# A streaming encoder step: TensorE's seven rounds of the recurrence as a loop or written out, and the order in which slots of the weight stream are asked for

## The reference

```python
def step(S, inp):
    r_t, d_t, k_t, v_t, kk_t, b_t = inp
    sa = jnp.einsum('bhvk,bhk->bhv', S, kk_t)
    S = S * d_t[:, :, None, :] - sa[..., None] * b_t[:, :, None, :] + v_t[..., None] * k_t[:, :, None, :]
    return S, jnp.einsum('bhvk,bhk->bhv', S, r_t)
```

## Time and profile before

| | us |
|---|---|
| median of 3 runs | 3645.53 |
| lowest, highest | 3642.49, 3646.55 |
| the profiled execution | 3655.61 |
| its span, first to last instruction | 3654.1 |
| TensorE busy in it | 3442.9 |
| VectorE, ScalarE, GpSimd busy | 1739.2, 1428.2, 42.0 |
| bytes read from HBM | 657.58 MB |

### The profile page before, as it was taken

The page is one execution under the profiler, slowest core; times in us unless marked ns, Lnnn a source line. Parts: engine busy times, 40 slices in busy tenths (PEclk is TensorE's granted clock), DMA queues, the critical chain, the costliest instruction groups (busy, mean ns, idle before and its releaser), DMA issues.

```text
span 3654.1 us, 82837 instructions
## 1 busy us (share of the span) xinstructions
PE 3442.9 (94%) x32728; PEld 3147.8 (86%) x32728; DVE 1739.2 (48%) x2888; ACT 1428.2 (39%) x2289; POOL 42.0 (1%) x81
## 2 busy tenths in 40 slices
PE   7899988888899999999999988999998999999997
PEld 3699977777788899899898967899898999999997
DVE  3443446555535444444444445554555544445453
ACT  2333335444425323323333255433435434334342
POOL 0000000000000000000000000000000000000000
PEclk8999999898999999999999999999999999999999
DMA  8777720000275777777777733234243544445452
GB/s 353 277 282 281 281 88 15 15 15 15 69 296 202 272 291 267 283 285 263 282 270 271 290 132 98 87 126 134 87 132 118 171 161 166 165 163 164 158 168 82
DMA packets 181337, 664.70 MB, mean 182 GB/s; under 512 B 21191, under 2 KB 21361, under 8 KB 180497
## 3 DMA queue, kind: packets, MB, share of 16 engines
q1 hardware_dynamic: 177840, 652.27, 50.2%
q0 software_dynamic: 3296, 9.48, 0.9%
HBM read 657.58 MB, written 4.09 MB: 181 GB/s over the span
## 4 chain that ended last, share of the span: by engine, by line
PE 83%; DMA 5%; issue 4%; DVE 3%; ACT 3%; SPq 1%; DVEq 0%; ACTq 0%; POOL 0%; POOLq 0%
PE ps L1614 21%; PE ps L1616 20%; PE ps L1615 20%; PE ps L1715 6%; DMA sb_raw<-stream 5%; PE ps L1598 4%; PE ps L1722 2%; PE ps L1661 1%; DVE sb_wlo L979 1%; SPq L440 1%; PE ps L1687 1%; PE ps L2006 1%; PE ps L2004 1%; PE ps L2005 1%; ACT sb_whi L571 1%
## 5 line engine op out<-in xcount | busy, mean ns | idle before, releaser
L979 DVE TENSOR_TENSOR sb_wlo<-sb_raw,sb_whi 128x1024 fp32r<-128x1024 f32 x778 | 940.9, 1223 | 948.8 <-ACT sb_whi L571 938.0
L571 ACT ACTIVATE sb_whi<-sb_raw 128x1024 fp32r<-128x1024 f32 x778 | 814.2, 1058 | 1296.5 <-PE ps L1616 1241.3
L1614 PE MATMUL ps<-sb_ah,sb_whi 128*128 128x288 f32 x3728 | 1117.5, 300 | 33.1 <-DVE sb_al L1059 19.0
L1615 PE MATMUL ps<-sb_ah,sb_wlo 128*128 128x288 f32 x3728 | 1104.8, 296 | 0.0
L1616 PE MATMUL ps<-sb_al,sb_whi 128*128 128x288 f32 x3728 | 1100.9, 295 | 0.0
L1614 PEld LDWEIGHTS ps<-sb_ah,sb_whi 128*128 128x128 f32 x3728 | 703.9, 189 | 67.0 <-issue 53.9
L1616 PEld LDWEIGHTS ps<-sb_al,sb_whi 128*128 128x128 f32 x3728 | 706.8, 190 | 0.0
L1615 PEld LDWEIGHTS ps<-sb_ah,sb_wlo 128*128 128x128 f32 x3728 | 705.2, 189 | 0.0
L1614 PE MATMUL ps<-sb_bh,sb_whi 128*128 128x288 f32 x2048 | 609.3, 298 | 0.0
L1615 PE MATMUL ps<-sb_bh,sb_wlo 128*128 128x288 f32 x2048 | 604.1, 295 | 0.0
L1616 PE MATMUL ps<-sb_bl,sb_whi 128*128 128x288 f32 x2048 | 602.1, 294 | 0.0
(11 more groups left out here) (264 smaller groups left out, 3314.4 us busy)
## 6 DMA issues: line engine op xcount, KB each, us to landing
sb_raw<-stream SPq DMA_DIRECT2D x1226, 512.0 KB, 5.2
sb_x<-xT SPq DMA_DIRECT2D x1, 2304.0 KB, 15.7
sb_x<-xT POOLq DMA_DIRECT2D x1, 2304.0 KB, 9.8
yT<-sb_x SPq DMA_DIRECT2D x1, 2304.0 KB, 6.9
sb_lwa<-lw POOLq DMA_DIRECT2D x16, 130.0 KB, 2.5
sb_lwg<-lw POOLq DMA_DIRECT2D x16, 130.0 KB, 2.5
sb_l1g<-l1g SPq DMA_DIRECT2D x2, 1024.0 KB, 19.7
wkvT<-sb_st POOLq DMA_DIRECT2D x16, 64.0 KB, 2.9
```

What stands on the lines that cost most here:

```text
L571: nc.scalar.activation(whi[:, q % SPL, :], raw[:, n % RAW, :], ACT.Copy).then_inc(hi_ready, 1)
L979: nc.vector.tensor_tensor(wlo[:, q % SPL, :], raw[:, n % RAW, :], whi[:, q % SPL, :], ALU.subtract).then_inc(lo_ready, 1)
L1614: mm(out, wh, xh, start=start, stop=False)
L1615: mm(out, wl, xh, start=False, stop=False)
```

## The change

Two places. On SyncE, the single call for the first round of "o" and the loop with the default order become one loop in which vectors' places come first in every round, through the first round of "kvd". On TensorE, the hardware loop over seven turns becomes a Python loop: seven copies of the body, with `it` a plain number.

```diff
@@ -473,9 +473,8 @@
             sp.wait_ge(L[0]["free"], NITER + 1)
-            behind_both(BY["o"].n0 // RAW, True)
-            with sp.Fori(BY["o"].n0 // RAW + 1, BY["kvd"].n0 // RAW + 1) as i:
-                behind_both(i)
+            with sp.Fori(BY["o"].n0 // RAW, BY["kvd"].n0 // RAW + 1) as i:
+                behind_both(i, True)
             with sp.Fori(BY["kvd"].n0 // RAW + 1, NSLOTS // RAW) as i:
                 behind_products(i)
@@ -1904,7 +1903,8 @@
             beside(0, 0, None, 0)
-            rounds(pe, 0, NITER - 1, turn)
+            for it in range(NITER - 1):
+                turn(it)
             beside(1, NITER - 1, 0, NITER - 1)
             beside(None, 0, 1, NITER - 1)
```

## The result

The changed kernel takes 3590.1 us (median; 3588.4 to 3591.6) where the kernel before takes 3645.6 on the same chip: a ratio of 0.985 [0.983, 0.987], so 55.5 us less. The forecast was 3587, with a range of 3573 to 3613. The two profiled executions differ by more, 67.2 us of span (3654.1 to 3586.9).

A forecast was written before the change was run, and what follows sets the result against it. TensorE, busy 3442.9 of 3654.1 us, was taken as the bound, so only its pauses and low clock could give time. Writing out the loop (49 us) plus vectors first (10) made 59: 3587 us, range 3573 to 3613.

The forecast's parts named there:

- Edit 1: TensorE's recurrence loop written out: six jumps back and their lowered clock go, saving 49 us, range 23 to 58.
- The length of a half turn: Recurrence on TensorE: 26.5 us for each of 14 half turns without jumps, 371.0 in all, bounds 363.2 to 389.8.
- ScalarE's 1.2 us: Recurrence: TensorE waits 0.2 us at each of six former jumps for squares behind ScalarE's table load; bounds 0 to 8.
- the pause behind the loop: TensorE's 3.30 us pause at 989.11 may go, stay or come twice: 0 in the sum, 4 us either way.
- the 421.2 us: Profiled time of the 14 half turns in the kernel before, from which the new half turns' time was subtracted.
- Edit 2: Mixed stages: asking for vectors first removes TensorE's 10.5 us of waits for vectors' slots; 10 us gained, bounds -6 to 12.
- products have time to spare: Mixed stages: product loads asked for after vectors still come 1 to 4 us early, so their wait costs nothing.
- Edit 2 brings nothing: Rival: vectors land in time, but equal waits appear at the return of `x` or the products; 3597 us, chance 0.12.
- the pause stays: Rival: the recurrence's jump pause is a semaphore wait the view can't name, so unrolling doesn't remove it; 3635 us, chance 0.03.
- Products late: Rival: SyncE asks for products too late, TensorE waits in each of 36 groups; 3688 us at 14 us landing, chance 0.04.
- the two on straight code: Rivals: straight code stalls, half turns of 27.84 us, 3604, chance 0.13; fetching is hidden, halves of 25.94, 3578, chance 0.10.
- ScalarE's splits (line 571) waiting for DMA: Sign in the mixed stages that was to show the prediction wrong; no size given.

The follow-up runs named there:

- the unroll alone: Kernel before with only TensorE's seven recurrence turns written out, SyncE's old load order kept: 3603.5 us, ratio 0.9895.
- before again: The kernel before, unchanged, run and profiled a second time: 3646.9 us, ratio 1.0002.
- the shifted: Changed kernel with 128 already met waits put on TensorE ahead of its seven turns, moving the code behind them: 3601.2 us, ratio 0.9889 to the kernel before.
- the one with two: Changed kernel, but TensorE loops three times over a two-turn body plus one straight turn, two jumps instead of six: 3608.2 us, ratio 0.9911 to the kernel before.
- the first two experiments: Kernel before with only TensorE's turns written out (3603.5 us, ratio 0.9895), and with only SyncE's vectors-first load order (3628.0 us, ratio 0.9961).
- the holds: Changed kernel with SyncE's first product load of a burst held until TensorE has used two product slots (3602.4 us) or three (3735.8 us).
- held for three: Changed kernel with SyncE's first product load of a burst held until TensorE has used three product slots: 3735.8 us, ratio 1.0242 to the kernel before.

## Why the prediction was right, and where its terms were off

**The time held** (3587 against 3590), with two terms off in opposite directions and one at zero that was not.

**Edit 1, the half turns.** Right in mechanism, point by point: the "issue" item fell from 30.3 to 3.5 us (under 3 was said), the half turns are 26.7 us on average (373.6 / 14) where 26.5 plus 1.2 us in all were taken, the clock is 1.00 up to the end of the recurrence, and there are twelve instruction packets fewer (some ten were said). The length of a half turn, named as the weakest point, cost 1.4 us of error (373.6 - 371.0 - 1.2). ScalarE's 1.2 us were counted twice: its table load stands in the first turn too, from which the 26.5 was taken.

```profile
L690 ACT ACT_TABLE_LOAD  x7: 1283/1283/1283, 531.8 to 891.4; - x7
```

By the two profiles the edit brought 47.5 us of the 49 in the half turns.

By the ratio of the unroll alone it brought 38, with the pause behind the loop in it, so some 35 in the half turns. The mis-sized term is the 421.2 us it was subtracted from. The prediction saw that the profiled execution was 10 us above the median and wrote that if all of that sat in the jumps the gain would be 49, but kept 59. Much of it did sit there: of the four profiles of that code the first has the longest turns, and before again, at 3645.1 us of span, has 7.0 of the 9.0 us of difference in them. One profile can't show how much such a term varies from execution to execution. The gap between its time and the median was the one hint, and the slow half turn behind a jump the one item that another execution could give back. With 49 for the whole the forecast would have been 3597. The two terms below made up for much of the error, so that the forecast came within 3 us is partly luck.

**Edit 2.** Waits of 10.5 us were taken away, as expected, and SyncE's waits moved to the vectors' line, as expected, but they were worth 15.2 us in the profiles and 14 (9 to 19) by the ratio. The step that failed is "removed are the waits of TensorE for vectors' slots, 10.5 us": idle as the rows show it is less than what a late slot costs, 1.01 against 1.37 us in the block above. By the profiles the stated bound of 12 was too low. That products have time to spare held: asked for 3.2 us in (2.9 said), landed at 10.6 (10.2), split at 13.0 (12.5). The return of `x` cost nothing: no wait of line 1613 for it remains but the 1.8 us, as today.

**The pause behind the loop** (0 taken, 4 either way) went: 3.3 us gained. It is there in all five profiles with jumps kept and in none of the straight ones but the shifted (1.77). It ends 1.3 to 1.5 us after an instruction packet has landed, as the short ones do, so it is a wait for code, and that packet is late. In the kernel before it starts at 986.72, when 454 matmuls and weight loads have begun since the start of the one before it at 974.90 (the row below counts those under way at its ends too). The usual distance is about 240; here it is 450 to 454 in the four profiles with six jumps and 396 in the one with two.

```profile
974.90:986.72 11.82, 8.87 (x234) 8.11 (x229) 3.20 (x8) 3.05 (x8) 0.00 (x0) 1.00 0.89 320
```

SyncE's burst of eight loads starts at 975.04, and its queue takes nearly all of the 16 DMA engines' time from 976 to 986:

```profile
q1 hardware_dynamic: 943, 3.47, 97.6%
```

That the burst is what holds the packet up is an argument from the times and was not tested.

**The rivals.** "Edit 2 brings nothing" and "the pause stays" fell with the first two experiments. "Products late" fell with the change itself, and the holds show between which two latenesses it begins. The prediction counted its cost in 36 groups; held for three, nearly every one of the 72 half groups takes 0.8 us or more longer. Of the two on straight code neither came: the second halves run from 25.9 to 28.3 us, the first from 26.2 to 27.1, with 5.4 us of short pauses up to the first loads of the output product. The fetching of straight code is not hidden then (5.3 to 9.3 us of such pauses up to 950 us in the kernels without a jump), nor does it make every half turn one of 27.84. The rule of the Trainium skill (Runtime: NRT & Kernel Launch, Instruction fetch mechanics) is borne out for the taken branch, by two packets and a pause of 4.2 to 4.7 us each, and not for straight code. By that rule the result would have been 3578.

**A wrong sign.** The prediction named ScalarE's splits (line 571) waiting for DMA in the mixed stages as a sign of failure. They do, for 611.0 us in 164 waits, and nothing is lost. Loads are asked for later relative to their slot's release, ScalarE is idle in any case (40% busy), and the split is done 4 us before TensorE wants it. A wait on an engine with slack is no sign; the wait of TensorE behind it would have been, and there is none.

**Left open:** why equal jumps cost differently, with a half clock of 3.4 to 13.7 us around them; what makes the packet behind the loop late; and why the kernel with two jumps has longer short pauses.

## What to carry to other kernels

On the engine that bounds the kernel, a loop with a long body (1,130 matmuls and as many weight loads here) costs about 6 us at each jump back (6.0 in the kernel with two; 6.3 to 7.9 by the profiles with six), some 4 as a pause and the rest as a lowered clock behind it. Write such a loop out. Loops with short bodies cost no such pause here: a turn of the mixed groups has 260 matmuls and as many weight loads, and none of their jumps back has a pause of "issue". From 1237 to 1267 us, the length of one such turn in the kernel before, the instruction queue moves nothing, where a turn of the recurrence takes 11 packets. How long a body may be in between was not tried. A queue that issues loads should ask for slots in the order of their use, and how far a load may slip is read from the time between its landing and its use, not from who waits on the way. When a term of the sum is idle time or a clock, look at how it varies over its own repeats and between span and median before taking one profile's value, and size a late load by the distance between what stands around it.

## What the runs showed of the hardware that was not expected

The half clock around a pause of 4.2 to 4.7 us lasts from 3.4 to 13.7 us with the same code, and the half turn behind takes 27.7 to 30.3 us. 128 waits on a semaphore that is already met took at most 6.46 us on TensorE, 50 ns each, any fetching among them included. Pauses for which the profile names no cause end 1.2 to 1.7 us after an instruction packet has landed, in 135 cases of 137, so the instruction queue's packets name it. A load asked for alone landed in 3.3 us and the fifth of a burst of eight in 7.4, so that asking 5.5 us later brought the data only 1.4 us later.
